# A third column block of the first output projection, spread matmul by matmul between the steps of the delta rule's inverse and states

## The reference

```python
y_a = gla_mixer(...)               # gated linear attention
y_b = gated_deltanet_mixer(...)    # gated delta rule
y_c = pool_mixer(...)
y_d = forgetting_attention(...)
y = jnp.concatenate([y_a, y_b, y_c, y_d], axis=-1) @ w_out
x = x + g1 * y
```

```python
def step(S, inp):
    v_new = u_i - w_i @ S
    o = (q_i * exp(g_i)) @ S + a_i @ v_new
    S = S * exp(g_last) + (k_i * exp(g_last - g_i)).T @ v_new
```

## Time and profile before

| | us |
|---|---|
| median of 3 runs | 3372.08 |
| fastest and slowest | 3371.34, 3374.7 |
| span of the profiled execution | 3366.5 |
| TensorE busy in it | 2801.2 |
| VectorE busy in it | 1692.1 |
| ScalarE busy in it | 442.3 |
| GpSimd busy in it | 941.8 |

### The profile page before, as it was taken

The page is one execution under the profiler, slowest core; times in us unless marked ns, Lnnn a source line. Parts: engine busy times, 40 slices in busy tenths (PEclk is TensorE's granted clock), DMA queues, the critical chain, the costliest instruction groups (busy, mean ns, idle before and its releaser), DMA issues.

```text
span 3366.5 us, 25507 instructions
## 1 busy us (share of the span) xinstructions
PE 2801.2 (83%) x9182; PEld 1672.9 (50%) x9182; DVE 1692.1 (50%) x2515; ACT 442.3 (13%) x1038; POOL 941.8 (28%) x713
## 2 busy tenths in 40 slices
PE   5999877989999999999999996777766666666666
PEld 3444656578888886444548654333322222222222
DVE  6555465122211113454207658665676777777755
ACT  1000233020110100001107311000010001000000
POOL 2111100000000000000003107455666666566663
PEclk9999878899999999999999998888887878788888
DMA  9999420346544444554631249999999999999998
GB/s 378 362 398 397 160 88 31 125 151 254 205 151 150 150 152 152 175 174 159 210 108 51 77 155 412 384 416 417 391 401 422 421 422 408 422 421 422 422 422 351
DMA packets 250236, 922.80 MB, mean 274 GB/s; under 512 B 18779, under 2 KB 38435, under 8 KB 183843
## 3 DMA queue, kind: packets, MB, share of 16 engines
q0 software_dynamic: 99840, 637.57, 46.1%
q1 hardware_dynamic: 150037, 283.97, 24.7%
q10 hardware_dynamic: 272, 0.13, 0.0%
HBM read 918.41 MB, written 8.44 MB: 275 GB/s over the span
## 4 chain that ended last, share of the span: by engine, by line
PE 59%; DMA 22%; DVE 10%; POOL 4%; issue 3%; ACT 2%; POOLq 0%; DVEq 0%; ACTq 0%
PE ps L1332 18%; DMA arena<-in_peer_v,proj 12%; PE ps L1016 11%; PE ps L1357 8%; PE ps L1651 7%; DMA proj<-in_peer_v,proj 4%; DMA proj<-in_peer_u,proj 4%; PE ps L1141 3%; PE ps L1544 3%; PE ps L1628 2%; POOL arena L577 2%; DMA arena<-in_w_mod 2%; PE ps L1058 2%; DVE proj L2362 1%; DVE arena L2362 1%
## 5 line engine op out<-in xcount | busy, mean ns | idle before, releaser
L1651 PE MATMUL ps<-proj,gates 128*128 128x512 f32 x992 | 572.5, 741 | 386.1 <-DMA proj<-in_peer_v,proj 276.4
L1332 PE MATMUL ps<-hT,ring 128*128 128x256 f32 x2816 | 608.2, 379 | 1.5 <-ACT hT L616 1.5
L1651 PEld LDWEIGHTS ps<-proj,gates 128*128 128x128 f32 x992 | 231.9, 242 | 723.5 <-issue 606.4
L1332 PEld LDWEIGHTS ps<-hT,ring 128*128 128x128 f32 x2816 | 535.0, 190 | 74.9 <-issue 2.3
L2362 DVE CUSTOM_DVE_ANT_0 arena<-arena,yT 128x2048 f32<-128x2048 f32 x128 | 291.5, 2292 | 213.5 <-DMA arena<-in_peer_u,proj 213.0
L1016 PE MATMUL ps<-ring,hT 128*128 128x512 f32 (+2 forms) x960 | 376.7, 555 | 1.8 <-DVE arena L2102 1.8
L2362 DVE CUSTOM_DVE_ANT_0 proj<-proj,yT 128x2048 f32<-128x2048 f32 x128 | 292.1, 2292 | 119.6 <-DMA proj<-in_peer_u,proj 115.8
L577 POOL DMA_INDIRECT proj<-in_peer_u,proj x128 | 205.4, 1604 | 296.9 <-DVE proj L2355 133.9
L1016 PEld LDWEIGHTS ps<-ring,hT 128*128 128x128 f32 x960 | 175.3, 192 | 200.0 <-issue 197.9
L1651 PE MATMUL ps<-arena,gates 128*128 128x512 f32 x512 | 233.9, 599 | 39.2 <-DMA arena<-in_peer_v,proj 38.8
L577 POOL DMA_INDIRECT arena<-in_peer_u,proj x128 | 242.2, 1892 | 84.8 <-DVE proj L2362 50.0
(11 more groups left out here) (449 smaller groups left out, 3023.1 us busy)
## 6 DMA issues: line engine op xcount, KB each, us to landing
arena<-in_w_mod POOLq DMA_DIRECT2D x96, 1024.0 KB, 10.2
ring<-in_w_in SPq DMA_DIRECT2D x52, 1024.0 KB, 10.3
ring<-in_ffn_w_gate SPq DMA_DIRECT2D x44, 1024.0 KB, 5.0
ring<-in_ffn_w_up SPq DMA_DIRECT2D x44, 1024.0 KB, 5.0
ring<-in_ffn_w_down SPq DMA_DIRECT2D x88, 512.0 KB, 4.9
ring<-in_w_out SPq DMA_DIRECT2D x16, 1024.0 KB, 5.7
ring<-in_w_out SPq DMA_DIRECT2D x32, 512.0 KB, 4.9
ring<-in_peer_wq SPq DMA_DIRECT2D x16, 1024.0 KB, 16.7
```

Of the source, the lines that this page charges most:

```text
L1332: ins = pe.matmul(ps[:, 4 * m + f, 0:T], ring[:, s, k, P * f:P * (f + 1)], hT[:, KS * s + k, :], start=(s == 0 and k == 0), stop=(s == SLO ...
L1651: ins = pe.matmul(ps[:, 4 * t + b, :], diag[:, j, :], row_slots[n % ROWS][:, NB * b:NB * (b + 1)], start=(h == 0 and j == 0), stop=(h == H ...
```

## The change

The 24 matmuls of units 6, 7 and 8 (block 2, the parts 3, 2 and 0) no longer run in one piece after the delta rule. `out1_ahead(n)` issues the next n of them, and is called between the steps of the inverse and of the states: once with 1 after each of the levels 1 to 4, with 2 after level 5, with 2 after L1285, with 2 after the output of each of the chunks 0 to 2, with 1 after L1295 of each of the chunks 1 to 3, and with 2 after the last output, ahead of `head_norm`. These are 19 matmuls; the other 5 are issued right after `head_norm`. They gather in banks 2 and 3. Each unit's first matmul waits for its slot, and its last one counts `unit_used`.

`OUT1` is reordered so that the parts 3, 2 and 0 of block 3 are units 9 to 11, and the delta rule's parts are the last four units, 12 to 15. The wait for `mix_out` 4 now stands ahead of unit 12. The banks are exchanged: blocks 2 and 0 finish in banks 2, 3 and blocks 3 and 1 in banks 0, 1 (`OUT1_BANK`). ScalarE and VectorE take block 2 out after unit 12 and block 3 after unit 13.

```diff
-OUT1 = (..., (2, 3), (2, 2), (2, 0), (2, 1), (3, 3), (3, 2), (3, 0), (3, 1), (0, 1), (1, 1))
-OUT1_LAST = ((2, 6, 10), (3, 10, 14), (0, 14, 15), (1, 15, 16))
+OUT1 = (..., (2, 3), (2, 2), (2, 0), (3, 3), (3, 2), (3, 0), (2, 1), (3, 1), (0, 1), (1, 1))
+OUT1_AHEAD = (6, 9)
+OUT1_LAST = ((2, 13), (3, 14), (0, 15), (1, 16))
+OUT1_BANK = lambda i: 2 * ((i + 1) % 2)
...
+        ahead = {"done": 0}
+
+        def out1_ahead(n):
+            for piece in range(ahead["done"], min(ahead["done"] + n, (OUT1_AHEAD[1] - OUT1_AHEAD[0]) * KS * NT)):
+                u, k, t = OUT1_AHEAD[0] + piece // (KS * NT), piece // NT % KS, piece % NT
+                if k == t == 0:
+                    pe.wait_ge(*at(f"slot{u % SLOTS}", 16 * (BLK["out1"] + u // SLOTS + 1)))
+                ins = pe.matmul(ps[:, OUT1_BANK(0) + t, :], yT[:, KS * OUT1[u][1] + k, P * t:P * (t + 1)], ring[:, u % SLOTS, k, :],
+                                start=(piece < NT), stop=False, skip_group_check=True)
+                if (k, t) == (KS - 1, NT - 1):
+                    ins.then_inc(sem("unit_used"), 1)
+                ahead["done"] = piece + 1
...
                 ins.then_inc(sem("inv_delta"), 1)
+            out1_ahead(2 if last else 1)
...
         ins.then_inc(sem("gdn_w"), 1)
+        out1_ahead(2)
...
                 ins.then_inc(sem("gdn_ws"), 1)
+                out1_ahead(1)
                 pe.wait_ge(*at("gdn_new", c))
...
             if c < 3:
                 ins.then_inc(sem("gdn_o"), 1)
+                out1_ahead(2)
         ins.then_inc(sem("mix_o"), 1)
+        out1_ahead(2)
         head_norm(1, gdn["sq"].rearrange("p a b -> p (a b)")[:, 0:1024])
 
-        for i, (b, first, end) in enumerate(OUT1_LAST):
+        out1_ahead(OUT1_AHEAD[1] * KS * NT)
+        for u in range(9, 12):
+            out1_unit(u, OUT1_BANK(1), start=(u == 9))
+        pe.wait_ge(*at("mix_out", 4))
+        out1_unit(12, OUT1_BANK(0), stop=True)
+        out1_unit(13, OUT1_BANK(1), stop=True)
+        for i in (2, 3):
             pe.wait_ge(*at("evac_act", EVB["out1"] + i + 1))
             pe.wait_ge(*at("evac_vec", EVB["out1"] + i + 1))
-            for u in range(first, end):
-                if u == 9:
-                    pe.wait_ge(*at("mix_out", 4))
-                out1_unit(u, 2 * (i % 2), start=(u == first), stop=(u == end - 1))
+            out1_unit(12 + i, OUT1_BANK(i), start=True, stop=True)
```

More of the change, by code:

```diff
@@ L48 @@
 EVB = {"in1": 0, "out1": 12, "in2": 16, "out2": 23}
-OUT1 = ((0, 3), (0, 2), (0, 0), (1, 3), (1, 2), (1, 0), (2, 3), (2, 2), (2, 0), (2, 1), (3, 3), (3, 2), (3, 0), (3, 1), (0, 1), (1, 1))
-OUT1_LAST = ((2, 6, 10), (3, 10, 14), (0, 14, 15), (1, 15, 16))
+OUT1 = ((0, 3), (0, 2), (0, 0), (1, 3), (1, 2), (1, 0), (2, 3), (2, 2), (2, 0), (3, 3), (3, 2), (3, 0), (2, 1), (3, 1), (0, 1), (1, 1))
+OUT1_AHEAD = (6, 9)
+OUT1_LAST = ((2, 13), (3, 14), (0, 15), (1, 16))
+OUT1_BANK = lambda i: 2 * ((i + 1) % 2)
 VEC = {
@@ L789, in residual_evac @@
             for i in range(4):
-                act.wait_ge(*at("unit_used", SLOTS * blk + OUT1_LAST[i][2]))
+                act.wait_ge(*at("unit_used", SLOTS * blk + OUT1_LAST[i][1]))
                 if i:
                     act.wait_ge(*at("added", i))
-                act.copy(ffn["y"][:, 0, :], ps[:, 2 * (i % 2), :]).then_inc(sem("evac_act"), 1)
+                act.copy(ffn["y"][:, 0, :], ps[:, OUT1_BANK(i), :]).then_inc(sem("evac_act"), 1)
                 if turned:
@@ L2033, in residual_add @@
             for i in range(4):
-                c, end = OUT1_LAST[i][0], OUT1_LAST[i][2]
+                c, end = OUT1_LAST[i]
                 r = slice(NB * c, NB * (c + 1))
                 vec.wait_ge(*at("unit_used", SLOTS * blk + end))
-                link(vec.tensor_tensor(ffn["y2"][:, 1, :], ps[:, 2 * (i % 2) + 1, :], gate[:, r], ALU.mult), "evac_vec")
+                link(vec.tensor_tensor(ffn["y2"][:, 1, :], ps[:, OUT1_BANK(i) + 1, :], gate[:, r], ALU.mult), "evac_vec")
                 link(vec.tensor_tensor(x[:, 1, r], x[:, 1, r], ffn["y2"][:, 1, :], ALU.add))
```

## The result

The changed kernel takes 3350.3 us in the median of 4 runs (3346.6 to 3352.4), against 3371.7 before: a ratio of 0.9933 (95% interval 0.9921 to 0.9945), 0.67% faster. Run again beside the later experiments it took 3346.2 us against 3371.3, a ratio of 0.9927 (0.9913 to 0.9940). The forecast was 3347.4. All nine runs lie between 3345.3 and 3352.4, with a median of 3347.1.

A forecast was written before the change was run, and what follows sets the result against it. TensorE bounds the projection behind `head_norm`; ahead of it the chain alternates with VectorE. 16.3 us removed, less 1.95 added, plus 10.5 for the clock, less 0.2, gives 24.7: 3372.1 to 3347.4 us, range for 8 in 10 3343 to 3358.

The forecast's parts named there:

- What bounds: Projection run behind `head_norm`: TensorE alone bounds it, so 19 of 24 matmuls leaving it take 16.3 us off the end.
- The cost beyond the cover: Inverse and states: pieces longer than the TensorE waits they fill add 1.95 us, bounds 1.5 and 4.
- The bound: Levels 1 to 4: +0 and +0.2 us each, the second if ScalarE's copy of L1271's product comes late by a hand-over.
- The clock: States, 588.68 to 616.16 us: with waits filled the clock stays at 2.4 GHz, gaining 10.5 us, bounds 0 and 10.5.
- The first rival: States: the clock falls all the same and pieces there take 1.70 us; gain 7.5 us, 3364.6 us; chance 0.07.
- The second: States: the clock falls for one or two chunks, about 3356 us; chance 0.10.
- the third: Inverse and states: wide and narrow work alternating loses the clock from 554 us until 616; +31.9 us, 3404 us; chance 0.02.
- What else moves: `mix_out` 4, ring loads, PSUM copies and the part after L1141: all covered or unchanged, 0 us, bounds 0 and +1.
- slot waits: Ring slots: three extra waits, all met, for which the sum takes 0.2 us off the gain.
- One of the signs named for a wrong prediction: After the projection: the prediction is wrong if the distance from L1141's end to the kernel's end grows.
- The sum: Whole change: 16.3 - 1.95 + 10.5 = 24.9 us, less 0.2 for slot waits, gives 24.7 us, 0.73% faster.
- The 5.6 us between the profiled span and the median: Whole kernel: the median of the runs lies 5.6 us above the profiled span, and the same goes for the changed kernel.

## Why the prediction was right

**What bounds.** As read: the projection's run behind `head_norm` was TensorE's alone, and what left it came off the end. The 19 pieces were put at 16.3 us; pieces that save no work against pieces that do differ by 16.4.

**The cost beyond the cover.** Forecast +1.95, bounds 1.5 to 4; it was about 2.6, if the clock gave its 10.5. From start to start the levels take 6.26 us instead of 6.18, +0.08 each where +0.03 was forecast: L1291 starts 1.78 us behind L1286, and the group behind that 0.94 later instead of 0.89. The bound had allowed for a late copy; the copy ends 0.1 us before L1291 starts, and whether it is the cause no run shows. The last level is +0.72 (577.96 to 581.52, against 575.47 to 578.31), forecast +0.56. From the first L1300 to L1319, with the two pieces behind u and w, it is 5.29 us as before, +0.0 as forecast. Chunk 0 takes 3.50 us (586.81 to 590.31) instead of 3.07, +0.43, forecast +0.44. Behind L1312 it is no more than before (1.90 us to L1319, where it was 2.01). In all the way from the first L1271 to `head_norm` it is 6.2 us shorter (65.9 to 59.7), where 8.8 - 1.95 = 6.85 was forecast.

**The clock.** It stayed at 2.4 GHz, as taken, and this was the step with most at stake. From chunk 1's L1301 to the start of the projection behind `head_norm` it was 27.48 us and is 18.14 (592.21 to 610.35): 9.3 less, where 10.5 for the clock less 0.85 for the pieces gives 9.65. The two runs with a part of the pieces show that either part alone does not hold it: with the states' waits open it falls one chunk late, with the inverse's open it falls ahead of chunk 1 and comes back. The Trainium skill, "TensorE: Matmul & The Clock Gate", section "A second HAM failure mode: psum-queue depth-cycling", puts the swings of the clock in another kernel down to frequent short idle times between groups of matmuls; the trace agrees, since no wait in the stretches ahead of the falls was above 1.7 us, and filling them kept the clock even with 16.3 us of useless work. All that was filled in here is 512 columns wide, and so no run tells whether it is the idle time gone or the wide matmuls that keep the clock. The first rival (the clock falls all the same, 3364.6) is out. The second, a fall for a chunk or two, came about only where pieces were left out. One reading of the third was wrong: wide matmuls have not only gone with the high level, since L1200, as wide, took 0.85 us a record at 0.50. It served as an argument against the slow case alone, and the forecast does not rest on it.

**What else moves: nothing,** as forecast; the run with the order alone took 1.0003 of before. `mix_out` 4 came 8.5 us behind `head_norm`'s start, and no wait stands ahead of unit 12. The 0.2 us that the sum takes off for slot waits has no row behind it, and no idle time shows at the first piece of a unit. One of the signs named for a wrong prediction did appear: from the end of L1143 to the end of the kernel it took 2685.1 us instead of 2681.5, and 2682.3 in the second profile. That is no more than the scatter told of below.

**The sum.** Forecast 24.9 us for the stage, measured 24.2; 24.7 in the time, measured 21.4 and then 25.1. Of the 0.7 us short of 24.9, 0.4 are those of the levels above and 0.3 are behind chunk 1's L1319, less 0.1 gained behind chunk 1's L1312. The other few us are not in the stage. The first group of transposes of the inverse started at 541.9 to 544.4 us in the ten profiled executions, and the part from the feed-forward layer to the end took 2666.0 to 2669.6 us, with no order by what was changed; the changed kernel's first profile had both long, and so its span is only 18.5 us shorter. Its first median, 2.9 above the forecast, is of four runs that scatter by 5.9 us; the median of all nine is 0.3 below the forecast. That the number came so near is in part luck.

**One reading was wrong, and cost nothing.** The 5.6 us between the profiled span and the median I took for time outside the span. In the changed kernel the profiled execution's own time is 3349.96 us and its span 3348.0, 2.0 us apart. So before's profiled execution was itself about 3.6 us quicker than its median. Because I took only the difference of the two kernels from the trace, the forecast is the same.

## What to carry to other kernels

Independent matmuls that are ready early are worth more as single pieces in the waits of a serial chain than as a block behind it: they save their own time, and a wait that is a little too short for the piece costs only the remainder. Count the cover from start to start of TensorE's groups, with the late restart after each wait, and look at the granted clock of the stretch. Where it reads 0.50 among many short waits, the pieces can pay a second time, by what the chain itself gains at full clock: here 7.8 us for pieces that saved no work. Where it reads 0.50 at the chain's beginning, try the first pieces ahead of it; here that gave 3.4 us for two.

## What the runs showed that I had not expected

- The clock rose sooner by more than the lead that TensorE was given. Two wide matmuls ahead of the inverse had the clock up by the time the inverse began (0.82 in the mean from 546 to 551 us, where it was 0.50). They start 2.8 us sooner behind the transposes than L1286 did, and the clock is up 4.9 us behind the transposes' start instead of 9.2, thus 4.3 sooner. The first level went from 7.46 to 5.40 us: I had put up to 1.4 us on it and it gave 2.1.
- In the run without the pieces behind L1312 one wait of 0.85 us stayed open in each chunk of 6.4 us, and the clock read 1.00 throughout (TensorE busy for 21.45 of 24.0 us). In the run with pieces in the inverse only, both waits of each chunk stayed open (1.07 or 1.31 us and 0.85) with no wide matmul in the states, and the clock fell in chunk 2.
- Work that is thrown away can pay: 16.3 us more of matmuls made the kernel 0.29% faster.
- The stage's last transposes (L992) always begin behind a wait of 7.7 us and took 5.05 to 6.46 us, by where in them the clock came back (2.8 us behind their start in the shortest, 5.7 in the longest). It makes 1.4 us of scatter, with no order by what was changed.
